# Output projection's first two tiles: the half of their products that reads the recurrence's and the delta rule's features is moved into the block before

## The chip, the cores and the metric

The kernel runs on one core of one Trainium2 chip. The metric is the device time in microseconds (us) of the whole program, median of three runs. TensorE (PE in the rows, PEld for its weight loads) multiplies; VectorE (DVE), ScalarE (ACT), GpSimd (POOL) and the DMA queue of SyncE (SP) work beside it.

## The reference, cut to what matters

Two decoder layers over 512 prompt tokens and 8 sequences of 4 sample tokens, width 1024, all in float32. Each layer computes

```python
z = x @ w_in                       # split among four mixers of 256 columns each
y_m = mLSTM, y_r = retention       # chunked mixers; each ends in a head norm and a gate
y_g = RG-LRU, y_w = RWKV-7         # linear recurrence; delta rule
mix = concat([y_m, y_r, y_g, y_w]) @ w_out
x = layer_norm(ALPHA * x + mix)    # then cross attention and a squared-ReLU MLP, alike
```

The row of `mix` of one token is a sum over 1024 features. 512 of them are the chunked mixers' (A is mLSTM, B retention), 256 the linear recurrence's (C), 256 the delta rule's (D).

## The kernel before, in words

Each layer is written as two blocks of five instruction streams, one for each engine. A block ends for all engines together: none begins the next block's stream before the last has ended the former's. Semaphores order the work inside a block.

The first block makes the features. They lie transposed, feature on the partition and the 544 tokens along the row, in eight tiles of 128 features: `Y = [z(f) for f in (6, 7, 14, 15, 18, 19, 20, 21)]`. Indices 0 and 1 are A's, 2 and 3 B's, 4 and 5 C's, 6 and 7 D's. C's and D's tiles are final when the semaphores `yC` and `yD` are up, D's during the loop over the chunks of A and B. The block's end on TensorE is the transpose of some state columns (L1143), then `head_means` and `head_variances` of A and B, each a product with a matrix of 1/64 (the helper's line is L585). Behind them ScalarE takes the eight variance halves out of PSUM with a logarithm (L1620) and makes the inverse roots (L1739), and VectorE multiplies A's and B's heads with them and with their gains and gates (L1569, L1571). Nothing else is left to do in the block then.

The second block begins with `project_tensor`. `w_out` is in the weight ring by then, as slabs 11 and 12, one for each half of 512 output columns. First it multiplies the 32 sample tokens (`part`, L1998): eight products for each half, four of which lie beside each other in groups of 32 columns of the array. Then come the four tiles of 128 prompt tokens (T0 to T3), for each half eight products of 128x128 by 128x512 that are summed in one PSUM bank (L2006). A float32 product is two records in the trace. Behind T0 the sample rows are folded (L2012); behind T1, T2 and T3 earlier tiles are transposed as soon as VectorE has normalised them (`turn_x_tensor`, L313). VectorE adds `ALPHA * x` to each half as its bank is full (`residual`, L2042), takes the moments (L287, L291) and normalises in two steps (L295, L297). It needs x back for that: SyncE's queue loads it at the start of the second block from the output tensors where the first block had parked it (L2631, L2632), then the norm's gain and bias (L323, L324), and then keys and values for the attention.

PSUM has eight banks; `bk.begin` waits until the bank's last reader has given it back. The variances of A lie in banks 0 to 3, those of B in banks 4 to 7.

Of the kernel before, what the change touches and what calls it, by code (L numbers as in the profile page):

```python
# [12 lines left out]
KC = D // P  # L13
DEPTH = 2
SEQ = 512
NB = 8
TS = 4
NS = NB * TS
NT = SEQ + NS
# [6 lines left out]
W512 = 512  # L26
# [13 lines left out]
TILES = [(0, 128), (128, 128), (256, 128), (384, 128), (SEQ, NS)]  # L40
# [179 lines left out]
def build(nc, A, O, table, where):  # L220

    with ExitStack() as ctx:
# [8 lines left out]
        tmp = sb("tmp", TMP)  # L231
# [3 lines left out]
        psum = ctx.enter_context(nc.psum_tensor("psum", [P, 8, 512], F32))  # L235

        def const(name, *shape):
            a, n = where[name]
            v = con[:, a:a + n]
            if len(shape) == 2:  # L240
                v = v.rearrange("p (a b) -> p a b", a=shape[0])
            return v

        def cols(t, at, *shape):
            n = 1
            for s in shape:
                n *= s
            v = t[:, at:at + n]
            if len(shape) == 2:
                v = v.rearrange("p (a b) -> p a b", a=shape[0])  # L250
            if len(shape) == 3:
                v = v.rearrange("p (a b c) -> p a b c", a=shape[0], b=shape[1])
            if len(shape) == 4:
                v = v.rearrange("p (a b c d) -> p a b c d", a=shape[0], b=shape[1], c=shape[2])
            return v

        def z(f, n=1):
            v = big[:, f * NT:(f + n) * NT]
            return v if n == 1 else v.rearrange("p (n t) -> p n t", n=n)
# [6 lines left out]
        wring = cols(ring, 0, 2, KC, W512)  # L266
# [39 lines left out]
        def turn_x_tensor(pe, bk, sig, ln, T, at, banks):  # L306

            t0, n = TILES[T]
            pe.wait_ge(sig["ln_done"], 5 * ln + at + 1)
            for g in range(2):  # L310
                ps = bk.begin(pe, ("xT", ln, T, g), banks[g]).rearrange("p (c t) -> p c t", c=4)
                for c in range(4):
                    ins = pe.transpose(ps[:, c, :n], xk[:n, T, (4 * g + c) * P:(4 * g + c + 1) * P], ident[:n, :n])  # L313
                bk.filled(ins, ("xT", ln, T, g))
# [34 lines left out]
        sig = Signals(nc, ctx, "")  # L349
        bk = Banks(sig, psum)  # L350
        for l in range(DEPTH):
            sig.layer()
            bk.layer()
            LN0, LN1, LN2, LN3 = range(3 * l, 3 * l + 4)
# [201 lines left out]
            def slab_wait(eng, n):  # L556

                if n < 2:
                    eng.wait_ge(sig[f"first{n}"], 16 * (l + 1))
                elif n == 17:  # L560
                    eng.wait_ge(sig["slab_up"], sig.at("slab_up", 16))
                else:
                    eng.wait_ge(sig[f"slab{n % 2}"], sig.at(f"slab{n % 2}", 16 * (n // 2 - (n > 17 and n % 2))))


            def slab_pe(pe, n):

                slab_wait(pe, n)
                return up_first if n == 17 else wring[:, n % 2, :, :]
# [144 lines left out]
                sp.dma_start(con[:, n_first:], table[:, n_first:]).then_inc(sig.dma("con"), 16)  # L714


            with nc.Block() as block:

                @block.tensor
                def _(pe):  # L720
# [9 lines left out]
                    ps = bk.begin(pe, ("prow",), 4)  # L730
                    bk.filled(pe.transpose(ps[:, :N_ROWS], prow[:N_ROWS, :], ident[:N_ROWS, :N_ROWS]), ("prow",))
                    ps = bk.begin(pe, ("prow2",), 5)
                    bk.filled(pe.transpose(ps[:, :64], prow2[:64, :], ident[:64, :64]), ("prow2",))
                    pe.wait_ge(sig["Sraw"], sig.at("Sraw", 16 * NB))
                    for pr in range(2):
                        ps = bk.begin(pe, ("SsT", pr), 6 + pr).rearrange("p (b c) -> p b c", b=4)
                        for b4 in range(4):
                            ins = pe.transpose(ps[:, b4, :], Sraw[:, b4, 2 * pr:2 * pr + 2, :].rearrange("p a b -> p (a b)"), ident)
# [3 lines left out]
                    if l == 0:  # L742
                        pe.wait_ge(sig["mem"], 16)
                        for nt in range(2):
                            for g in range(2):
                                ps = bk.begin(pe, ("memT", nt, g), 6 + g).rearrange("p (c t) -> p c t", c=4)
                                for c in range(4):
                                    k = 4 * g + c
                                    ins = pe.transpose(ps[:, c, :], mems[:, nt, k * P:(k + 1) * P], ident)
# [29 lines left out]
                    ps = bk.begin(pe, ("orow1",), 6)  # L779
# [11 lines left out]
                    for T in range(5):  # L791
                        t0, n = TILES[T]
                        pe.wait_ge(sig["dfeat"], sig.at("dfeat", 1))
                        for i, pair in enumerate(((X2, X4), (z(ZK_D, 2), z(ZV_D, 2)))):
                            ps = bk.begin(pe, ("dtok", T, i), 4 + i).rearrange("p (a c) -> p a c", a=4)
                            for j in range(2):
                                for pr in range(2):
                                    ins = pe.transpose(ps[:n, 2 * j + pr, :], pair[j][:, pr, t0:t0 + n], ident)
# [4 lines left out]
                        for i, left in enumerate((X4, z(ZK_D, 2))):  # L803
                            if i:
                                spare_products(pe, ("dsc", T), 4, (0, 1))
                            ps = bk.begin(pe, ("dsc", T, i), 6 + i).rearrange("p (q a s t) -> p q a s t", q=2, a=2, s=2)
                            for pr in range(2):
                                for c in own_chunks:
                                    tc = slice(t0 + c.start, t0 + c.stop)
                                    w = c.stop - c.start  # L810
                                    ins = pe.matmul(ps[c, pr, :, :, :w], left[:, pr, tc], dpad[:, pr, :, :, c], start=True, stop=True)
# [3 lines left out]
                        for li, m in enumerate(levels):  # L815
# [3 lines left out]
                            ps = bk.begin(pe, ("X", T, m), 2)[:, 0:256].rearrange("p (h t) -> p h t", h=H)  # L819
# [3 lines left out]
                            for h in range(H):  # L823
                                for c in own_chunks:
                                    w = c.stop - c.start
                                    ins = pe.matmul(ps[c, h, :w], om[c, h, :w], (const("ident64") if m == 1 else Dm[:, h, :])[c, :w],
                                                    start=True, stop=True)
# [5 lines left out]
                            if not last:  # L833
                                ps = bk.begin(pe, ("D", T, m), 3)[:, 0:256].rearrange("p (h t) -> p h t", h=H)
                                for h in range(H):
                                    for c in own_chunks:
                                        w = c.stop - c.start
                                        ins = pe.matmul(ps[c, h, :w], DmT[c, h, :w], Xm[c, h, :w], start=True, stop=True)
                                bk.filled(ins, ("D", T, m))
                            ps = bk.begin(pe, ("DT", T, m), 4)[:, 0:256].rearrange("p (h t) -> p h t", h=H)  # L840
                            for h in range(H):
                                for c in own_chunks:
                                    w = c.stop - c.start
                                    ins = pe.matmul(ps[c, h, :w], Xm[c, h, :w], DmT[c, h, :w], start=True, stop=True)
# [4 lines left out]
                        ps = bk.begin(pe, ("CV", T), 6)[:, 0:256].rearrange("p (h v) -> p h v", h=H)  # L849
# [7 lines left out]
                        if T < 4:  # L857
# [8 lines left out]
                            ps = bk.begin(pe, ("UV", T), 7)[:, 0:256].rearrange("p (h v) -> p h v", h=H)  # L866
# [125 lines left out]
                    def head_variances(pre, sq, bank):  # L992

                        pe.wait_ge(sig[pre + "sq"], sig.at(pre + "sq", 1))
                        for i in range(2):
                            product(pe, (pre + "var", i), bank + i, lambda k: sq[:, i, :], [const("mean64")])
# [148 lines left out]
                    head_means("B", z(ZQ_B, 2), 4)  # L1145
                    head_variances("A", X2, 0)
                    head_variances("B", X4, 4)


                @block.vector  # L1150
# [830 lines left out]
            up_first = cols(big, 16 * NT + 4096, KC, W512)  # L1981
            KEY_BANKS = (0, 1, 3)
            pvs = cols(tmp, 10260, W256)
            Y = [z(f) for f in (6, 7, 14, 15, 18, 19, 20, 21)]


            partial = cols(tmp, 10698, 2, W512)
            PROJ_ORDER = (0, 4, 1, 2, 3)


            def project_tensor(pe, pre, left, slabs, ln):

                w = [slab_pe(pe, n) for n in slabs]
                for half in range(2):
                    ps = bk.begin(pe, (pre, "part", half), half)
                    for k in range(KC):
                        g = (k % 4) * NS
                        ins = pe.matmul(ps[g:g + NS, :], left[k][:, SEQ:NT], w[half][:, k, :], start=(k < 4), stop=(k >= 4),  # L1998
                                        skip_group_check=True)
                    bk.filled(ins, (pre, "part", half))  # L2000
                for T in range(4):
                    t0, n = TILES[T]
                    for half in range(2):
                        ps = bk.begin(pe, (pre, T, half), 2 * ((T + 1) % 2) + half)
                        for k in range(KC):
                            ins = pe.matmul(ps[:n, :], left[k][:, t0:t0 + n], w[half][:, k, :], start=(k == 0), stop=(k == KC - 1))  # L2006
                        bk.filled(ins, (pre, T, half))
                    if T == 0:
                        for half in range(2):
                            bk.given(pe, (pre, "part", half))  # L2010
                            ps = bk.begin(pe, (pre, 4, half), 6 + half)
                            bk.filled(pe.matmul(ps[:NS, :], const("fold"), partial[:, half, :], start=True, stop=True), (pre, 4, half))  # L2012
                    if T == 1:
                        turn_x_tensor(pe, bk, sig, ln, 0, 0, (4, 5))
                    if T == 2:
                        turn_x_tensor(pe, bk, sig, ln, 4, 1, (4, 5))
                        turn_x_tensor(pe, bk, sig, ln, 1, 2, (4, 5))
                    if T == 3:
                        turn_x_tensor(pe, bk, sig, ln, 2, 3, (4, 5))


            def project_scalar(s, pre, ln):
# [272 lines left out]
            with nc.Block() as block:  # L2295

                @block.tensor
                def _(pe):
                    project_tensor(pe, "wout", Y, (11, 12), LN1)

                    pe.wait_ge(sig["kpt"], sig.at("kpt", 16))
                    for nt in range(2):
# [431 lines left out]
```

## Time and profile before

| what | us |
|---|---|
| median of the runs (2537.10 to 2543.14) | 2538.28 |
| the profiled execution | 2533.99 |
| its span, first to last instruction | 2532.0 |
| TensorE busy in it | 2406.4 |
| idle time of TensorE ahead of the projection, layer 0 | 9.05 |
| the same, layer 1 | 9.04 |

A time at the left of a timeline row counts from the start of the span. A row shows its start, its length, engine, line and operation, what it writes and reads, and how many records it joins; the bracket is the idle time before it and what ended it. In a row of stretches each engine has its busy time and its records in brackets; the clock beside them is 1.00 for TensorE's 2.4 GHz and 0.50 for 1.2 GHz.

### The profile page before, as it was taken

The page shows a single profiled execution, that of the slowest core. Times are in us where ns is not written, and L with a number is a line of the kernel's source. Part 1 is how long each engine was busy: PE and PEld are TensorE (multiplying, and loading weights), DVE is VectorE, ACT ScalarE, POOL GpSimd, SP SyncE. Part 2 cuts the span into 40 slices and gives each one's busy share as a digit, 9 for nine tenths or more (in the row PEclk, how much of TensorE's full clock was granted, in tenths as well). Part 3 has the DMA queues.
Part 4 walks back from the last instruction along what each step waited for, and adds up shares of the span by engine and source line. Part 5 has one row for each costly group of instructions (what it writes and reads, how often), then busy time and mean ns, then how long its engine had stood idle before and what let it go on. Part 6 is the DMA issues. An engine that isn't in the chain of part 4 may idle for free. (4 is left out here: it accounts for less than half of the span.)

```text
span 2532.0 us, 31605 instructions
## 1 busy us (share of the span) xinstructions
PE 2406.4 (95%) x13470; PEld 1761.3 (70%) x13470; DVE 811.9 (32%) x1617; ACT 465.6 (18%) x983; POOL 110.9 (4%) x208
## 2 busy tenths in 40 slices
PE   7989998979999999999989899989899999999997
PEld 6867674545874888888877666655458658888886
DVE  4242233544033644000132422436321345430012
ACT  2331122011121222000023321220112212220000
POOL 0011100100000000000001011000000000000000
PEclk9999998979999999999999999989799999999999
DMA  7111003253233112222231111023433331212220
GB/s 268 64 37 36 6 30 88 72 175 117 106 140 135 65 67 100 67 67 67 68 117 67 34 36 35 23 86 100 139 133 112 139 133 40 94 67 90 77 67 36
DMA packets 137674, 215.05 MB, mean 85 GB/s; under 512 B 35528, under 2 KB 69632, under 8 KB 137408
## 3 DMA queue, kind: packets, MB, share of 16 engines
q1 hardware_dynamic: 135232, 208.84, 24.4%
q10 hardware_dynamic: 2304, 4.20, 0.4%
q8 instruction: 108, 1.77, 0.3%
q14 instruction: 30, 0.25, 0.0%
HBM read 198.43 MB, written 14.58 MB: 84 GB/s over the span
## 5 line engine op out<-in xcount | busy, mean ns | idle before, releaser
L2137 PE MATMUL psum<-big,ring 128*128 128x288 f32 (+1 forms) x2048 | 471.2, 393 | 0.0
L2137 PEld LDWEIGHTS psum<-big,ring 128*128 128x128 f32 x2048 | 388.5, 190 | 79.9 <-DMA ring<-in_w_down 0.4
L585 PE MATMUL psum<-xT,ring 128*128 128x256 f32 (+1 forms) x1536 | 357.8, 394 | 8.4 <-DMA ring<-in_w_in 6.0
L585 PEld LDWEIGHTS psum<-xT,ring 128*128 128x128 f32 x1536 | 291.9, 191 | 69.8 <-DMA ring<-in_w_in 6.2
L632 PE MATMUL psum<-xT,ring 128*128 128x256 f32 (+1 forms) x768 | 223.5, 418 | 0.1
L2080 PE MATMUL psum<-tmp 128*128 128x272 f32 x768 | 181.4, 393 | 0.0
L2080 PEld LDWEIGHTS psum<-tmp 128*128 128x128 f32 x768 | 145.8, 190 | 30.8 <-issue 0.8
L632 PEld LDWEIGHTS psum<-xT,ring 128*128 128x128 f32 x768 | 134.3, 192 | 41.4 <-issue 15.2
L331 DVE SCALAR_TENSOR_TENSOR xtok<-xtok,psum 128x256 f32<-128x256 f32 (+1 forms) x40 | 16.3, 407 | 442.4 <-PE psum L2071 421.3
L629 PE MATMUL psum<-ring,ext 128*128 128x512 f32 x256 | 120.0, 610 | 4.5 <-ACT ext L1600 4.5
L2412 PE MATMUL psum<-ring,big 128*128 128x512 f32 x256 | 113.1, 595 | 0.0
L2006 PE MATMUL psum<-ring,big 128*128 128x512 f32 x256 | 111.6, 594 | 0.0
L2080 PE MATMUL psum<-xT,ring 128*128 128x272 f32 x448 | 107.2, 392 | 0.0
L1593 ACT ACTIVATE big<-psum 128x256 f32<-128x256 f32 (+1 forms) x112 | 44.4, 396 | 320.5 <-PE psum L585 197.2
L2080 PEld LDWEIGHTS psum<-xT,ring 128*128 128x128 f32 x448 | 85.0, 190 | 17.4
L2265 ACT ACTIVATE tmp<-psum 128x256 f32<-128x256 f32 (+1 forms) x32 | 12.7, 398 | 450.5 <-PE psum L2137 450.5
L2006 PEld LDWEIGHTS psum<-ring,big 128*128 128x128 f32 x256 | 48.0, 190 | 60.8 <-issue 60.8
L629 PEld LDWEIGHTS psum<-ring,ext 128*128 128x128 f32 x256 | 47.5, 194 | 58.6 <-issue 54.7
L2412 PEld LDWEIGHTS psum<-ring,big 128*128 128x128 f32 x256 | 47.4, 190 | 56.9 <-issue 56.9
L2042 DVE SCALAR_TENSOR_TENSOR xtok<-xtok,psum 128x512 f32<-128x512 f32 (+1 forms) x40 | 27.3, 682 | 140.4 <-PE psum L2006 86.5
L2080 PE MATMUL psum<-xT,tmp 128*128 128x272 f32 x256 | 63.9, 392 | 0.0
L2242 ACT ACTIVATE big<-psum 128x272 f32<-128x272 f32 x32 | 12.7, 398 | 267.8 <-PE psum L2080 267.8
(449 smaller groups left out, 2693.8 us busy)
## 6 DMA issues: line engine op xcount, KB each, us to landing
ring<-in_w_down SPq DMA_DIRECT2D x16, 2048.0 KB, 8.2
ring<-in_w_in SPq DMA_DIRECT2D x14, 2048.0 KB, 8.5
ring<-in_w_up SPq DMA_DIRECT2D x14, 2048.0 KB, 7.9
big<-in_cache_mem_k SPq DMA_DIRECT2D x16, 1024.0 KB, 5.4
ring<-in_xa_wk SPq DMA_DIRECT2D x4, 2048.0 KB, 8.1
ring<-in_xa_wv SPq DMA_DIRECT2D x4, 2048.0 KB, 10.1
ring<-in_w_out SPq DMA_DIRECT2D x4, 2048.0 KB, 8.9
tmp<-in_cache_mem_v SPq DMA_DIRECT2D x8, 1024.0 KB, 10.0
```

The lines of the kernel that those rows point to most:

```text
L331: ins = v.scalar_tensor_tensor(x, x, ALPHA, ps[:n, (T % 2) * W256:(T % 2) * W256 + W256], ALU.mult, ALU.add)
L585: ins = pe.matmul(ps[:m, :w], lhsT_list[k], rhs(k)[:, c], start=(k == 0), stop=(k == n - 1))
L629: ins = pe.matmul(bank, memT[:, k, half * P:(half + 1) * P], wring[:, n % 2, k, :], start=(k == 0), stop=(k == KC - 1))
L632: ins = pe.matmul(bank[:, :c.stop - c.start], wring[:, n % 2, k, i * P:(i + 1) * P], xTv[:, k, c], start=(k == 0), stop=(k == KC - 1))
L1593: bk.give(act(z(f)[:, c], ps[:, 0:c.stop - c.start], fn, scale=scale), ("z", f, half))
L2006: ins = pe.matmul(ps[:n, :], left[k][:, t0:t0 + n], w[half][:, k, :], start=(k == 0), stop=(k == KC - 1))
L2042: bk.give(v.scalar_tensor_tensor(x, x, ALPHA, ps[:n, :], ALU.mult, ALU.add), key)
L2080: ins = pe.matmul(ps[:, :HT], left[:, k, :], right[:, k, :], start=(k == 0), stop=(k == KH - 1))
L2137: ins = pe.matmul(ps, w[r][:, k, i * P:(i + 1) * P], hT[:, 2 * KC * r + k, c], start=(r == 0 and k == 0), stop=(r == 1 and k == 2 * KC - 1))
L2242: bk.give(s.activation(hT[:, 2 * u + 1, T_HALVES[0]], ps[:, :HT], ACT.Copy), ("up", u, 0))
L2265: bk.give(s.activation(yT[q % 2][:, i, c], ps[:, :c.stop - c.start], ACT.Copy), ("down", q, i, half))
L2412: ins = pe.matmul(ps, aT[:, k, t0:t0 + n], w[:, k, :], start=(k == 0), stop=(k == KC - 1))
```

## The change

The order of the work on TensorE changes, and the banks. `wout_ahead` is called at the end of the first block, behind `head_variances`: for T0 and T1, both halves, it multiplies the features 4 to 7 (C and D) and leaves the sums open in their banks. In the second block `wout_tensor` takes the place of `project_tensor`: `part` first, then for T0 and T1 the features 0 to 3 that are still missing, and T2 and T3 with all eight, 4 to 7 first. The folds and transposes keep their places between the tiles. T0 and T2 use banks 2 and 3, T1 and T3 banks 0 and 1, `part` banks 4 and 5 (before: 0 and 1). No product is added or left out, and the streams of the other engines are as they were.

```diff
+            WOUT_BANKS = ((2, 3), (0, 1), (2, 3), (0, 1))
+            def wout_tile(pe, T, ks):
+                t0, n = TILES[T]
+                for half in range(2):
+                    w = wring[:, (11 + half) % 2]
+                    key = ("wout", T, half)
+                    if key not in bk.turn:
+                        bk.begin(pe, key, WOUT_BANKS[T][half])
+                    ps = psum[:, bk.turn[key][0], :]
+                    for k in ks:
+                        ins = pe.matmul(ps[:n, :], Y[k][:, t0:t0 + n], w[:, k, :], start=(k == 4), stop=(k == 3))
+                    if ks[-1] == 3:
+                        bk.filled(ins, key)
+
+            def wout_ahead(pe):
+                for half in range(2):
+                    slab_wait(pe, 11 + half)
+                pe.wait_ge(sig["yC"], sig.at("yC", 1))
+                pe.wait_ge(sig["yD"], sig.at("yD", 1))
+                for T in range(2):
+                    wout_tile(pe, T, range(4, KC))
+
+            def wout_tensor(pe):
+                for half in range(2):
+                    ps = bk.begin(pe, ("wout", "part", half), 4 + half)
...
+                for T in range(4):
+                    wout_tile(pe, T, range(4) if T < 2 else (4, 5, 6, 7, 0, 1, 2, 3))
...
                     head_variances("A", X2, 0)
                     head_variances("B", X4, 4)
+                    wout_ahead(pe)
...
-                    project_tensor(pe, "wout", Y, (11, 12), LN1)
+                    wout_tensor(pe)
```

## Rows read from the trace of the kernel before

**Rows 1.** The page's first part: busy time, share of the span, instructions.

```profile
PE 2406.4 (95%) x13470; PEld 1761.3 (70%) x13470; DVE 811.9 (32%) x1617; ACT 465.6 (18%) x983; POOL 110.9 (4%) x208
```

**Rows 2.** Timeline of TensorE's products in layer 0.

```profile
540.97 3.99 PE L585 MATMUL psum<-tmp,con 128*128 128x256 f32 x16
554.01 6.09 PE L1998 MATMUL psum<-ring,big 128*32 128x512 f32 x32 [9.05 <-PEq L717]
560.03 14.00 PE L2006 MATMUL psum<-ring,big 128*128 128x512 f32 x32
573.96 1.91 PE L2012 MATMUL psum<-tmp,con 128*32 128x512 f32 x4
575.79 14.00 PE L2006 MATMUL psum<-ring,big 128*128 128x512 f32 x32
```

**Rows 3.** Timeline of all engines in layer 0's idle time.

```profile
542.71 4.12 ACT L1620 ACTIVATE tmp<-psum,con 128x256 f32<-128x256 f32 x8
...
552.05 1.48 DVE L1571 SCALAR_TENSOR_TENSOR big<-big,tmp 128x544 f32<-128x544 f32 x2
553.82 0.40 SPq L2631 DMA_DIRECT2D xtok<-out_y_prompt  x1
```

**Rows 4.** Timeline of TensorE's products in layer 1.

```profile
1798.78 1.08 PE L585 MATMUL psum<-tmp,con 128*128 128x256 f32 x4
1808.89 5.00 PE L1998 MATMUL psum<-ring,big 128*32 128x512 f32 x32 [9.04 <-PEq L717]
1813.82 14.00 PE L2006 MATMUL psum<-ring,big 128*128 128x512 f32 x32
```

**Rows 5.** Stretches of 1 us: PE, PEld, DVE, ACT, POOL, clock, DMA share, GB/s.

```profile
549.00:550.00 1.00, 0.00 (x0) 0.00 (x0) 0.96 (x2) 0.00 (x0) 0.00 (x0) 0.50 0.00 0
...
559.00:560.00 1.00, 1.00 (x12) 0.13 (x4) 0.00 (x0) 0.00 (x0) 0.00 (x0) 1.00 1.05 430
...
1804.00:1805.00 1.00, 0.00 (x0) 0.00 (x0) 0.96 (x3) 0.00 (x0) 0.00 (x0) 0.93 0.00 0
...
1811.00:1812.00 1.00, 1.00 (x9) 0.24 (x5) 0.00 (x0) 0.00 (x0) 0.00 (x0) 0.66 0.91 348
```

**Rows 6.** DMA packets between 545 and 554 us.

```profile
DMA packets 0, 0.00 MB, mean 0 GB/s; under 512 B 0, under 2 KB 0, under 8 KB 0
```

**Rows 7.** TensorE around the border between the layers.

```profile
1266.14 0.82 PE L2071 MATMUL psum<-con,tmp 128*128 128x128 f32 x6
1272.92 8.57 PE L585 MATMUL psum<-xT,ring 128*128 128x256 f32 x32 [5.96 <-DMA ring<-in_w_in]
```

**Rows 8.** SyncE's queue in layer 0, ahead of the idle time.

```profile
502.64 10.07 SPq L404 DMA_DIRECT2D ring<-in_w_out  x2
```

**Rows 9.** SyncE's queue in layer 1, the second block's start.

```profile
1809.14 0.50 SPq L2632 DMA_DIRECT2D xtok<-out_y_sample  x1
...
1810.15 1.23 SPq L324 DMA_DIRECT2D tmp<-in_ln_b  x1
```

**Rows 10.** DMA issues in the same stretch: count, size, us to landing.

```profile
tmp<-in_ln_b SPq DMA_DIRECT2D x1, 512.0 KB, 10.8
xtok<-out_y_sample SPq DMA_DIRECT2D x1, 128.0 KB, 9.4
```

**Rows 11.** Timeline of VectorE at T0's second half, layer 0.

```profile
574.14 0.69 DVE L2042 SCALAR_TENSOR_TENSOR xtok<-xtok,psum 128x512 f32<-128x512 f32 x1 [6.18 <-PE psum L2006]
574.86 1.29 DVE L287 BATCH_NORM_STATS2 sm<-xtok 128x6 f32<-128x512 f32 x2
576.18 0.21 DVE L291 BATCH_NORM_AGGREGATE sm<-sm 128x2 f32<-128x12 f32 x1
576.43 1.28 DVE L295 SCALAR_TENSOR_TENSOR xtok<-xtok,sm,tmp 128x1024 f32<-128x1024 f32 x1
577.75 1.28 DVE L297 SCALAR_TENSOR_TENSOR xtok<-xtok,sm,tmp 128x1024 f32<-128x1024 f32 x1
```

**Rows 12.** Behind the projection: the second pair of key transposes, layers 0 and 1.

```profile
624.47 1.97 PE L2307 MATMUL psum<-con,tmp 128*128 128x128 f32 x8 [2.70 <-ACT big L2553]
...
1878.26 1.15 PE L2307 MATMUL psum<-con,tmp 128*128 128x128 f32 x8 [2.69 <-ACT big L2553]
```

**Rows 13.** Stretches of 2 us in layer 0, columns as in rows 5.

```profile
518.00:520.00 2.00, 2.00 (x4) 0.37 (x3) 1.03 (x2) 0.00 (x0) 0.00 (x0) 0.50 1.05 410
...
624.00:626.00 2.00, 1.53 (x7) 1.54 (x8) 1.03 (x1) 1.28 (x3) 0.00 (x0) 0.50 1.05 401
```

More of the change, by code:

```diff
@@ L714, in first_loads @@
                 sp.dma_start(con[:, n_first:], table[:, n_first:]).then_inc(sig.dma("con"), 16)
+            Y = [z(f) for f in (6, 7, 14, 15, 18, 19, 20, 21)]
+            partial = cols(tmp, 10698, 2, W512)
+            WOUT_BANKS = ((2, 3), (0, 1), (2, 3), (0, 1))
[11 more added lines that the diff above has]
+                        bk.filled(ins, key)
@@ new lines, in wout_ahead @@
+            def wout_ahead(pe):
[8 more added lines that the diff above has]
+                    ps = bk.begin(pe, ("wout", "part", half), 4 + half)
+                    for k in range(KC):
+                        g = (k % 4) * NS
+                        ins = pe.matmul(ps[g:g + NS, :], Y[k][:, SEQ:NT], wring[:, (11 + half) % 2, k, :], start=(k < 4), stop=(k >= 4),
+                                        skip_group_check=True)
+                    bk.filled(ins, ("wout", "part", half))
+                for T in range(4):
+                    wout_tile(pe, T, range(4) if T < 2 else (4, 5, 6, 7, 0, 1, 2, 3))
+                    if T == 0:
+                        for half in range(2):
+                            bk.given(pe, ("wout", "part", half))
+                            ps = bk.begin(pe, ("wout", 4, half), 6 + half)
+                            bk.filled(pe.matmul(ps[:NS, :], const("fold"), partial[:, half, :], start=True, stop=True), ("wout", 4, half))
+                    if T == 1:
+                        turn_x_tensor(pe, bk, sig, LN1, 0, 0, (4, 5))
+                    if T == 2:
+                        turn_x_tensor(pe, bk, sig, LN1, 4, 1, (4, 5))
+                        turn_x_tensor(pe, bk, sig, LN1, 1, 2, (4, 5))
+                    if T == 3:
+                        turn_x_tensor(pe, bk, sig, LN1, 2, 3, (4, 5))
@@ L1983, in build @@
             pvs = cols(tmp, 10260, W256)
-            Y = [z(f) for f in (6, 7, 14, 15, 18, 19, 20, 21)]
-            partial = cols(tmp, 10698, 2, W512)
             PROJ_ORDER = (0, 4, 1, 2, 3)
[L1991 to L2019, printed above, removed]
             def project_scalar(s, pre, ln):
```

## The prediction

> **What bounds the kernel.** I read the busy shares first: TensorE works 95% of the span, no other engine over 32% [rows 1]. So time is TensorE's products plus the places where it stands, and a reordering pays only where it fills such a place. Next the timeline of TensorE around the edited code. In layer 0 the variances end at 540.97 + 3.99 = 544.96, and the projection's first product starts at 554.01, after 9.05 us idle, released by the end of the block and not by data [rows 2]. Layer 1 repeats it with 9.04 us [rows 4]. Then the other engines in that gap: ScalarE takes the eight variance halves until 546.83, and VectorE's last gate product ends at 552.05 + 1.48 = 553.53; the first instruction of the next block, a load, follows at 553.82 [rows 3]. The chain of head norms therefore sets the gap, and TensorE has no part in it after 544.96.
>
> Last the stretches of 1 us, for the clock. It stands at 0.50 (1.2 GHz) from 549.00 and is back at 1.00 (2.4 GHz) from 559.00; in layer 1 it falls near 1804.9 and is back near 1811.7 (the 0.66 of that stretch is 0.68 us low and 0.32 us full) [rows 5]. So the first products after the gap run at half speed: the gap costs more than its length.
>
> **What is removed, moved and added.** Moved are 2 tiles x 2 halves x 4 features = 16 products, 32 records. T0's 32 records before start at 560.03 and what follows them starts at 573.96: 13.93 us [rows 2]. The same number of records now stands at the end of the first block, in each layer.
>
> *Do they start at once?* They need three things. The weights: both `w_out` slabs were issued between 502.64 and 512.7, over 30 us ahead [rows 8]. The features C and D: D's last write lies in the chunk loop, before the means. And free banks: T0 takes 2 and 3, which ScalarE drains as second and fourth of its eight reads, 4.12 / 8 = 0.515 us each, so at 542.71 + 1.03 = 543.74 and 544.77; the product that wants bank 2 comes at 544.96, the one for bank 3 half a tile (3.5 us) later [rows 2, 3]. I cost the start at nothing.
>
> *The end of the block.* TensorE now ends last, at 544.96 + 13.93 = 558.9, where VectorE still ends at 553.53: its chain hangs on the variances, which are issued before the moved products. The 9.05 us disappear, and the overhang of 4.9 us is work that has left the second block, so it costs nothing. What stays is the border itself. Its price with TensorE as the last engine is in no row. Below: 0.29 us, from VectorE's end to the next load [rows 3]. Above: TensorE's own end at 1266.14 + 0.82 = 1266.96 to its next product at 1272.92, 5.96 us, put down to a weight load [rows 7]. VectorE's end to TensorE's start was 0.48 us; the case is nearest to that one, and I take 0.6.
>
> A rule speaks for the upper end. The Trainium skill, "Runtime: NRT & Kernel Launch", section on instruction fetch mechanics, says that a taken branch to a page that isn't loaded stalls the engine until a DMA has brought it. In the old order such a fetch could have hidden in the 9 us. The trace speaks against it: between 545 and 554 not one DMA packet moves, instruction queues included [rows 6]. The page gives no time for such a stall, so by it the sum would only be worse by an unstated amount, between my two bounds.
>
> *The clock.* `part` took 560.03 - 554.01 = 6.02 us in layer 0, of which 5.0 low: at full clock 2.5 + 1.0 = 3.5. In layer 1 it took 4.93 us, of which 2.8 low: 1.4 + 2.1 = 3.5 too [rows 2, 4, 5]. With TensorE standing for 0.6 us in place of 9, behind 13.9 us of wide products, I expect the clock to stay at 2.4 GHz. Gain 2.5 us and 1.4 us; bound on the other side nothing.
>
> *The reload, which is now late.* All loads of the second block start behind the border, some 5.4 us later than before, while `part` and T0 are shorter by 2.5 + 7 us. Take S as the block's first product. T0's first half is full at S + 3.5 + 3.5 = S + 7. The sample rows of x are issued 0.25 us after S and land 9.4 us later, S + 9.65; the norm's bias 1.26 us after S and 10.8 us later, S + 12.1 (layer 1, the later one) [rows 4, 9, 10]. VectorE so waits some 3 us for x, which it didn't before. The second half is full at S + 10.5, and from its residual add to the end of the norm it is 577.75 + 1.28 - 574.14 = 4.9 us [rows 11]: S + 15.5. TensorE asks for T0's transposes after `part` 3.5, T0 7.0, fold 1.8 (573.96 to 575.79) and T1 7.0, at S + 19.3. So 3.8 us are left and I cost the reload at nothing. If the loads were later than that, each us would be a us, at this transpose. T4 and T1 come up behind T2's 14 us, T2 behind T3's 14: as before. The attention's weights are released by T3, its first keys are wanted 60 us in; they move with TensorE.
>
> *Banks in the second block.* `part` takes 4 and 5, free since 546.9; T2 takes T0's, read by VectorE at S + 11.3, long before. Nothing.
>
> **Sum.** Layer 0: 9.05 + 2.5 - 0.6 = 10.95. Layer 1: 9.04 + 1.4 - 0.6 = 9.85. Together 20.8 us. The profiled execution took 2533.99 us (2532.0 of span and 2.0 around it), so 2513.2. The median of the runs shown stands 4.3 us above that execution; the same offset gives 2517.5.
>
> **Rivals.**
> - *The border costs more when TensorE ends last* (code fetched, drain). For: no row shows it, and the rule above. Against: the empty DMA stretch. At its bound, 5.96 in place of 0.6 twice, 10.7 us are lost: 2528. From 3 us each on it is 2522. Chance 0.08.
> - *The clock gives nothing back*, since it falls anyway around the border. For: in layer 0 a wait of 2.70 us was enough for 0.50 at 624 to 626, and the transposes there took 1.97 us, which in layer 1 took 1.15 [rows 12, 13]. Against: the pause is now 0.6. Then 3.9 us are missing: 2521.5. Chance 0.07.
> - *The gap reappears at T0's transpose*, because x comes late. It begins when the norm is over 3.8 us later than worked out; at some 14 us later in each layer the gain is gone and the time is the old one, beyond it slower. For: the loads are the only thing that starts later. Against: landings of 9.4 and 10.8 us are measured ones under the same load. Partial stall 0.03, no change 0.02.
> - *The other side: the clock is low under the moved products.* A busy TensorE doesn't suffice: at 518 to 520 it was busy throughout, with narrow products, at 0.50 [rows 13]. At 1.2 GHz the moved records would take 27.9 us and `part` 7.0. Per layer the piece from the variances to T0's old length is then 27.9 + 0.6 + 7.0 = 35.5 against 9.05 + 6.02 + 13.93 = 29.0, or 28.0 in layer 1: 14 us slower in all, 2552. It decides from about 21 us of low clock in a layer. Against: these products are 128x512 over the full array, and the 64 records of T0 and T1 took 14.00 us each, at full clock. Chance 0.02.
>
> The forecast itself has 0.78. Within it: the border from 0.29 to 2 us, and the clock's falls elsewhere (a shift of all that follows can add or take one, some 1 us each), with the spread of the median (2537.1 to 2543.1): 2512 to 2522. To hold 8 in 10 with the bounds I give 2511 to 2526, which takes in the clock rival and most of the border's. Less than 0.3% (7.6 us), about what a measurement of this kernel can tell from no change, needs a loss of 13 us out of 20.8: same 0.03, slower 0.02, faster 0.95.
>
> **What would show it.** In the profile after: products of the projection directly behind the variances, 13.9 us, without a wait; an idle time of about 0.6 us at the block's end; clock 1.00 through `part`, which takes 3.5 us; VectorE's first residual add waiting for the load; T0's transposes without idle time before them; all later groups as before. It is wrong if the border takes over 2 us, if a stretch at 0.50 lies in `part` or in the moved products, or if a wait stands before T0's transposes.

## The result and the profile after

| | median us | runs | ratio to before, 95% interval |
|---|---|---|---|
| before | 2539.20 | 6 | |
| changed | 2519.79 | 6 | 0.9921 [0.9905, 0.9936] |
| changed, second set | 2522.88 | 5 | 0.9933 [0.9920, 0.9947] |
| changed, third set | 2522.56 | 5 | 0.9924 [0.9909, 0.9938] |

The change is 17 to 20 us faster, clear of noise in all three sets. The forecast was 2517.5 us in a range of 2511 to 2526, and a sum of 20.8 us, a ratio of 0.9918.

The timeline of TensorE's products in layer 0 after the change answers to [rows 2]. The moved and the remaining products of the prompt tiles are L732 now, the sample rows L753, the fold L762, and the border of the blocks L772.

```profile
546.95 4.00 PE L585 MATMUL psum<-tmp,con 128*128 128x256 f32 x16
550.78 13.89 PE L732 MATMUL psum<-ring,big 128*128 128x512 f32 x32
564.98 3.64 PE L753 MATMUL psum<-ring,big 128*32 128x512 f32 x32 [0.30 <-PEq L772]
568.55 7.13 PE L732 MATMUL psum<-ring,big 128*128 128x512 f32 x16
575.61 1.91 PE L762 MATMUL psum<-tmp,con 128*32 128x512 f32 x4
577.45 7.13 PE L732 MATMUL psum<-ring,big 128*128 128x512 f32 x16
584.42 1.04 PE L313 MATMUL psum<-con,xtok 128*128 128x128 f32 x8
```

The 32 moved records follow the variances without a wait. At the border TensorE stands 0.30 us in place of 9.05, and the sample rows take 3.64 us in place of 6.09. Below, the piece of a layer is the stretch from the variances' first record to tile 0's transposes. In layer 0 it was 589.63 - 540.97 = 48.66 us and is 584.42 - 546.95 = 37.47; in layer 1 it was 47.75 and is 37.46. The ends of the pieces of before that [rows 2, 4] don't hold are these, layer 0 first:

```profile
589.63 1.04 PE L313 MATMUL psum<-con,xtok 128*128 128x128 f32 x8
...
1795.67 4.18 PE L585 MATMUL psum<-tmp,con 128*128 128x256 f32 x16
...
1843.42 1.04 PE L313 MATMUL psum<-con,xtok 128*128 128x128 f32 x8
```

Layer 1 of the changed kernel has the same picture as its layer 0:

```profile
1792.85 3.99 PE L585 MATMUL psum<-tmp,con 128*128 128x256 f32 x16
1796.68 13.89 PE L732 MATMUL psum<-ring,big 128*128 128x512 f32 x32
1810.87 3.64 PE L753 MATMUL psum<-ring,big 128*32 128x512 f32 x32 [0.30 <-PEq L772]
...
1830.31 1.04 PE L313 MATMUL psum<-con,xtok 128*128 128x128 f32 x8
```

The stretches of 1 us around the border, which answer to [rows 5]: the clock stays at 1.00 throughout.

```profile
564.00:565.00 1.00, 0.70 (x6) 0.05 (x5) 0.00 (x0) 0.06 (x1) 0.00 (x0) 1.00 0.00 0
565.00:566.00 1.00, 1.00 (x12) 0.45 (x16) 0.00 (x0) 1.00 (x1) 0.00 (x0) 1.00 0.00 0
...
568.00:569.00 1.00, 1.00 (x9) 0.30 (x2) 0.00 (x0) 0.32 (x1) 0.00 (x0) 1.00 1.03 418
```

VectorE in the same layer, against [rows 3, 11]. Its last gate product still ends ahead of the border, now by 5 us; its first residual add waits for the load of x and no longer for the product.

```profile
558.02 1.48 DVE L1627 SCALAR_TENSOR_TENSOR big<-big,tmp 128x544 f32<-128x544 f32 x2
574.08 0.69 DVE L2065 SCALAR_TENSOR_TENSOR xtok<-xtok,psum 128x512 f32<-128x512 f32 x1 [14.57 <-DMA xtok<-out_y_sample]
575.80 0.69 DVE L2065 SCALAR_TENSOR_TENSOR xtok<-xtok,psum 128x512 f32<-128x512 f32 x1 [1.04 <-PE psum L732]
...
579.41 1.28 DVE L297 SCALAR_TENSOR_TENSOR xtok<-xtok,sm,tmp 128x1024 f32<-128x1024 f32 x1
```

Tile 0 is normalised at 580.69, 3.7 us before its transposes are asked for at 584.42.

One thing doesn't fit at first sight: the two pieces gained 11.2 and 10.3 us, and yet this profile's span is 2520.7 us against 2532.0, only 11.3 less. The rest lies where the code was not changed. The first profile of before came to layer 0's variances at 540.97, this one at 546.95, and the stretches of the chunk loop show why. The rows are TensorE's busy time, records and so on, with the clock third from the end; the first fence is of the kernel before, the second of the changed one.

```profile
227.00:231.00 4.00, 4.00 (x26) 2.96 (x25) 0.69 (x1) 1.09 (x2) 0.39 (x1) 1.00 0.00 0
199.00:365.00 166.00, 159.86 (x1881) 115.74 (x1880) 38.20 (x99) 34.91 (x88) 21.08 (x38) 1.00 0.08 27
```

```profile
227.00:231.00 4.00, 4.00 (x19) 2.42 (x17) 0.00 (x0) 1.17 (x2) 0.00 (x0) 0.57 0.00 0
199.00:365.00 166.00, 159.86 (x1742) 114.19 (x1741) 36.22 (x94) 32.51 (x84) 21.05 (x38) 0.96 0.08 27
```

TensorE is busy alike, but at 0.96 of the clock it gets through fewer records in 166 us. That stretch ends 186 us ahead of the first moved product (550.78), so the product itself can't have caused it; whether it belongs to the changed kernel or to the execution is for the further profiles below to say.

### The profile page after: what moved, and what is told of

The parts are those of the page before. It is cut to its first block and busy times, and to the rows that moved or that the text cites. A ratio compares the mean times of both kernels' runs of the same rounds, so it can differ in the third digit from the quotient of the medians.

```text
span 2520.7 us, 31607 instructions
## 1 busy us (share of the span) xinstructions
PE 2412.5 (96%) x13470; PEld 1765.9 (70%) x13470; DVE 812.1 (32%) x1617; ACT 466.0 (18%) x983; POOL 110.7 (4%) x208
## 5 line engine op out<-in xcount | busy, mean ns | idle before, releaser
L585 PE MATMUL psum<-xT,ring 128*128 128x256 f32 (+1 forms) x1536 | 360.5, 396 | 8.4 <-DMA ring<-in_w_in 5.9
L585 PEld LDWEIGHTS psum<-xT,ring 128*128 128x128 f32 x1536 | 293.9, 192 | 70.6 <-DMA ring<-in_w_in 6.2
L632 PE MATMUL psum<-xT,ring 128*128 128x256 f32 (+1 forms) x768 | 228.2, 425 | 0.1
L632 PEld LDWEIGHTS psum<-xT,ring 128*128 128x128 f32 x768 | 137.6, 196 | 43.2 <-issue 16.1
L629 PE MATMUL psum<-ring,ext 128*128 128x512 f32 x256 | 119.3, 607 | 4.5 <-ACT ext L1656 4.5
L732 PE MATMUL psum<-ring,big 128*128 128x512 f32 x256 | 111.9, 594 | 0.0
L2103 PEld LDWEIGHTS psum<-xT,ring 128*128 128x128 f32 x448 | 85.0, 190 | 17.4
L732 PEld LDWEIGHTS psum<-ring,big 128*128 128x128 f32 x256 | 48.0, 190 | 60.0 <-issue 59.8
L629 PEld LDWEIGHTS psum<-ring,ext 128*128 128x128 f32 x256 | 47.5, 194 | 58.5 <-issue 54.7
```

Source lines behind the costliest of these rows:

```text
L585: ins = pe.matmul(ps[:m, :w], lhsT_list[k], rhs(k)[:, c], start=(k == 0), stop=(k == n - 1))
L629: ins = pe.matmul(bank, memT[:, k, half * P:(half + 1) * P], wring[:, n % 2, k, :], start=(k == 0), stop=(k == KC - 1))
L632: ins = pe.matmul(bank[:, :c.stop - c.start], wring[:, n % 2, k, i * P:(i + 1) * P], xTv[:, k, c], start=(k == 0), stop=(k == KC - 1))
L732: ins = pe.matmul(ps[:n, :], Y[k][:, t0:t0 + n], w[:, k, :], start=(k == 4), stop=(k == 3))
L2103: ins = pe.matmul(ps[:, :HT], left[:, k, :], right[:, k, :], start=(k == 0), stop=(k == KH - 1))
```

## The experiments

All ratios are against the kernel before, run on the same chip in the same rounds.

**The changed kernel again**, as a yardstick.

> The changed kernel once more, as the yardstick of this set. By the measured pieces of its first profile (11.2 us gained in layer 0 and 10.3 us in layer 1 between the variances and the transposes of tile 0) it is 20 to 21.5 us faster than the kernel before, ratio 0.9915 to 0.9925. If the four extra low-clock stretches in each layer's chunk loop of that profile belonged to the change and not to chance, they show again and the gain is nearer 11 us, 0.9957.

Measured 2522.88 us, 0.9933 [0.9920, 0.9947]. The pieces are 37.66 us in both layers. The chunk loop from 199 to 365 us ran at 1.00 this time:

```profile
199.00:365.00 166.00, 159.86 (x1858) 115.15 (x1856) 38.96 (x100) 32.59 (x85) 21.78 (x39) 1.00 0.08 27
```

So the extra low stretches of the first profile don't belong to the change. A kernel that moves nothing has them as well: the one with products for nothing (below) had 0.96 there.

**The same order behind the border.** The call is taken out of the first block and put at the start of the second.

```diff
                     head_variances("B", X4, 4)
-                    wout_ahead(pe)
...
             def wout_tensor(pe):
+                wout_ahead(pe)
```

> The same order and the same banks, but the 16 products stand behind the border of the blocks, as the first thing of the second block. The theory (the gain is the idle time ahead of the border): TensorE stands 9.05 us again and starts at 1.2 GHz, the time is that of the kernel before, ratio 0.998 to 1.002. The rival (the gain comes from the new order or the banks in the second block): 20 us faster here too, 0.992.

Measured 2544.70 us, 1.0022 [1.0012, 1.0032]. The gain is gone, so it comes from the place and neither from the order of the features nor from the banks. It is even 5.6 us slower than before (3.0 to 8.1 by the interval), just outside the expected 0.998 to 1.002. The timeline shows why:

```profile
559.25 17.01 PE L732 MATMUL psum<-ring,big 128*128 128x512 f32 x32 [9.30 <-PEq L773]
576.18 3.64 PE L754 MATMUL psum<-ring,big 128*32 128x512 f32 x32
```

The restart at 1.2 GHz now falls on the wide products, 17.01 us in place of 13.9, while the sample rows behind them take 3.64 us in place of 6.09 and 5.00. The pieces are 49.86 and 49.72 us, 1.2 and 2.0 more than in the first profile of before, and 2.0 and 1.9 more than in its second one. Together that is 3.2 or 3.9 us, which lies within the interval of the time.

**One layer only.** In layer 0 the call stands ahead of the border, in layer 1 behind it.

```diff
                     head_variances("B", X4, 4)
-                    wout_ahead(pe)
+                    if l == 0:
+                        wout_ahead(pe)
...
             def wout_tensor(pe):
+                if l:
+                    wout_ahead(pe)
```

> The products are ahead of the border in layer 0 alone, in layer 1 behind it. The theory: the layers add up, 11.2 us of gain, ratio 0.9955. The rival (the shift of everything behind layer 0 gives or takes as much as the place): anything from 0.992 to 0.999.

Measured 2533.73 us, 0.9968 [0.9956, 0.9980], 8.1 us (5.1 to 11.2). The pieces are 37.65 us in layer 0, as with the change, and 48.78 in layer 1: 11.0 gained and 1.0 lost against the first profile of before, 10.0 together. The expected 11.2 us had left out the loss in the layer in which the products stand behind the border. In the pieces the layers add up; the time alone allows that and the rival too, whose range (0.992 to 0.999) it lies in.

**One tile only.** Tile 0's products are ahead, tile 1 is computed whole in the second block.

```diff
-                for T in range(2):
+                for T in range(1):
                     wout_tile(pe, T, range(4, KC))
...
-                    wout_tile(pe, T, range(4) if T < 2 else (4, 5, 6, 7, 0, 1, 2, 3))
+                    wout_tile(pe, T, range(4) if T < 1 else (4, 5, 6, 7, 0, 1, 2, 3))
```

> Only tile 0's eight products, 6.95 us, are ahead. They fit in the 9.05 us, so VectorE ends the block again, at its old time. The theory: 6.95 us less behind the border in each layer, and the pause of some 2.6 us leaves the clock at 2.4 GHz, which gives the 2.5 and 1.4 us of the sample rows: 13.9 + 3.9 = 17.8 us faster, ratio 0.9930. If the clock falls in a pause of 2.6 us as well: 13.9 us, 0.9945. The rival (more moved is more gained in proportion): half of the change's gain, 10 us, 0.996.

Measured 2524.88 us, 0.9943 [0.9931, 0.9956], 14.5 us.

```profile
551.13 7.03 PE L732 MATMUL psum<-ring,big 128*128 128x512 f32 x16
560.17 3.64 PE L753 MATMUL psum<-ring,big 128*32 128x512 f32 x32 [2.02 <-PEq L772]
```

Half the products leave 2.02 us of idle time and the clock is kept all the same. The pieces are 39.38 and 39.37 us, 9.3 and 8.4 gained: 17.7, as the theory has it. Proportional gain (10 us) is out. The time of the whole program (interval 11 to 17.5 us) agrees with them only at its edge, and its ratio is nearer to the 0.9945 expected for a clock that falls. So it does not decide by itself whether the clock paid; the profile does, with 3.64 us for the sample rows in both layers.

**Products for nothing.** The kernel before, with eight wide products whose sum nobody reads, behind the variances.

```diff
                     head_variances("B", X4, 4)
+                    slab_wait(pe, 12)
+                    bk.given(pe, ("Avar", 0, 1))
+                    for k in range(KC):
+                        pe.matmul(psum[:, 2, :], z(18 + k % 4)[:, 0:P], wring[:, 0, k, :], start=True, stop=True)
```

> The kernel before, with eight 128x128 by 128x512 products (7 us) added at the end of the first block; nobody reads their result, and no work is moved. It measures the clock's part by itself. If the clock is a gain of its own, the sample rows take 3.6 us in place of 6.0 and 4.9: 3.8 us faster, ratio 0.9985. If only the idle time counts, or the clock falls anyway at the border: 1.0000.

Measured 2538.99 us, 0.9994 [0.9984, 1.0004].

```profile
554.06 7.03 PE L1151 MATMUL psum<-ring,big 128*128 128x512 f32 x16
563.25 3.64 PE L2002 MATMUL psum<-ring,big 128*32 128x512 f32 x32 [2.17 <-PEq L717]
```

In the profile the clock's part is there by itself: the sample rows take 3.64 us with no work removed, and the pieces are 46.20 and 46.39 us, 2.5 and 1.4 less than in the first profile of before. In the time of the whole program 3.8 us can't be told from nothing here: the interval reaches from 4.1 us faster to 1.0 slower.

**Three tiles.** Tile 2's second half of features goes ahead as well; its sums take banks 4 and 5, and `part` and the transposes behind T1 and T2 move to 6 and 7.

```diff
-            WOUT_BANKS = ((2, 3), (0, 1), (2, 3), (0, 1))
+            WOUT_BANKS = ((2, 3), (0, 1), (4, 5), (0, 1))
...
-                for T in range(2):
+                for T in range(3):
                     wout_tile(pe, T, range(4, KC))
```

> Tile 2's eight products are ahead as well, 7 us more in the first block in each layer. The theory: the gap is already full with two tiles, so nothing more is gained and the larger overhang costs nothing; tile 1's transposes are asked for 28.4 us into the second block and its norm is done at 26.7, so no new wait. As fast as the change, 20 to 21 us faster than before, 0.992. The rival (what is moved is gained): 34 us, 0.9865. The other rival (the overhang delays the loads and VectorE's later tiles): slower than the change by the wait, some us in each layer.

Measured 2520.65 us, 0.9914 [0.9901, 0.9928], within two of the three intervals of the change and overlapping the third. From the variances to tile 1's transposes it is 53.06 us in both layers, to 0.01 us what the first profile of the change has. With the gap full, 7 us more ahead of the border bring nothing and cost nothing:

```profile
551.42 20.76 PE L732 MATMUL psum<-ring,big 128*128 128x512 f32 x48
572.48 3.64 PE L753 MATMUL psum<-ring,big 128*32 128x512 f32 x32 [0.30 <-PEq L772]
```

**The reload late.** In SyncE's queue the keys and the first two value loads go ahead of x and of the norm's parameters.

```diff
-                    sp.dma_start(xk[:, 0:4, :], yp).then_inc(sig.dma("xres"), 16)
-                    sp.dma_start(xk[:NS, 4, :], ys).then_inc(sig.dma("xres"), 16)
...
                     v_load(0)
                     v_load(1)
+                    sp.dma_start(xk[:, 0:4, :], yp).then_inc(sig.dma("xres"), 16)
+                    sp.dma_start(xk[:NS, 4, :], ys).then_inc(sig.dma("xres"), 16)
```

The two loads of `ln_params` move with them.

> The changed kernel, with 3 MB of keys and values issued ahead of the reload of x and of the norm's parameters in SyncE's queue. At the 410 GB/s of the profile x lands 7.7 us later. In the profile of the change the norm of tile 0 is done 3.7 us before its transposes are asked for. The theory (slack of 3.7 us, then each us is a us): 4.0 us of wait in each layer, 8 us slower than the change, 12 us faster than before, 0.9953. The rival (the reload is hidden anyway): as the change, 0.992.

Measured 2528.92 us, 0.9949 [0.9937, 0.9962], 13 us faster than before and so 4 to 7 slower than the change. VectorE's first residual add starts at 581.17 in place of 574.08, 7.1 us later into the block, and 7.6 us later in layer 1. Now tile 0's transposes wait:

```profile
587.61 1.97 PE L313 MATMUL psum<-con,xtok 128*128 128x128 f32 x8 [3.03 <-DVE xtok L297]
589.37 15.94 PE L732 MATMUL psum<-ring,big 128*128 128x512 f32 x32
...
1834.40 1.09 PE L313 MATMUL psum<-con,xtok 128*128 128x128 f32 x8 [2.43 <-DVE xtok L297]
1835.33 13.90 PE L732 MATMUL psum<-ring,big 128*128 128x512 f32 x32
```

The waits are 3.03 and 2.43 us, less than the 4.0 expected. With the change the second half's add still stood 1.04 us (layer 0) and 1.36 us (layer 1) for its product after x had come; here it doesn't, so a late x can use that time besides the 3.7 us. That makes 4.8 and 5.1 us of slack; in layer 0 the norm then lost 0.81 us to its bias, which had been moved back with x. In layer 0 the clock fell behind the wait as well, and tile 2 took 15.94 us in place of 13.90. So the slack is real: beyond it a late reload is waited for, and may take the clock with it.

**One half earlier.** Four of the moved products, tile 0's first half, are issued while TensorE waits for VectorE in A's decode states; they take bank 7, and B's means and variances alternate in two banks to leave it free.

```diff
                         elif T == 4:
+                            if pre == "A":
+                                wout_early(pe)
...
-                        product(pe, (pre + "mu", i), bank + i, lambda k: ht[:, i, :], [const("mean64")])
+                        product(pe, (pre + "mu", i), bank + (i if pre != "B" else 0), lambda k: ht[:, i, :], [const("mean64")])
```

> The changed kernel, with four of the moved products (tile 0, first half) issued earlier still, where TensorE waits 2.10 us for VectorE's masked values of A's decode states; B's means and variances use two banks in turn in place of four. The theory: another 2.1 us of idle time is filled in each layer, and the norm chain, which ends 5 us before TensorE at the border, can take the delay: 4 us faster than the change, more if the wide products lift the clock there (0.50 for 24 us): 0.990 to 0.988. The rival: the norm chain becomes the later one again and gives it back, 0.992.

Measured 2519.06 us, 0.9911 [0.9897, 0.9924]: by the time alone not to be told from the change, nor from the 0.990 expected. The profile speaks against a gain.

```profile
515.02 2.82 PE L629 MATMUL psum<-ring,ext 128*128 128x512 f32 x6
...
531.76 6.60 PE L732 MATMUL psum<-ring,big 128*128 128x512 f32 x8
538.29 1.07 PE L1171 MATMUL psum<-big,tmp 32*64 32x512 f32 x4
540.23 2.21 PE L1171 MATMUL psum<-big,tmp 32*64 32x512 f32 x4 [0.86 <-DVE big L1570]
...
554.57 1.29 PE L585 MATMUL psum<-tmp,con 128*128 128x256 f32 x4 [1.26 <-ACT tmp L1683]
```

The 2.10 us wait is filled, but the eight records run almost wholly at 1.2 GHz there, 6.60 us in place of 3.5, and two new waits of 0.86 and 1.26 us come behind them. From the last value products (L629) to tile 0's transposes (585.90) layer 0 takes 70.88 us; with the change it is 515.45 to 584.42, 68.97. Layer 1 loses 1.9 us too (70.86 for 68.96). The norm chain does not end last either (the border's wait is still 0.30), so the rival's reason fails as well. Whether the theory of a gain fails stays open: the profiled execution is the slowest of the five (2522.82 us) and has the lowest granted clock (0.973), while the other four took 2515.88 to 2520.89 us at 0.976 to 0.977, more than any of the 16 executions of the changed kernel had (0.970 to 0.975). No profile shows where the clock was higher in them.

**Both kernels beside each other once more.**

> The kernel before under another name: a second profile of it, and what two equal kernels differ by in this measurement. Ratio 1.000, within 0.0015. Its piece from B's and A's variances to the transposes of tile 0 is 48.7 and 47.7 us again, give or take 1 us for the clock of the sample rows. If the first profile's 541 us up to there were luck, this one is nearer the 545 to 550 us of the other profiles.

Measured 2539.14 us, 0.9999 [0.9990, 1.0008]. Its pieces are 47.85 and 47.86 us. Here the clock was low for less of layer 0's sample rows than in [rows 2]:

```profile
558.37 5.09 PE L1998 MATMUL psum<-ring,big 128*32 128x512 f32 x32 [9.04 <-PEq L717]
```

And it came to layer 0's variances at 545.15, not at 540.97; from 199 to 365 us the clock was 0.98. So the same kernel differs by 4 us there from one execution to the next.

> The changed kernel beside the copy of the kernel before. By the pieces it is 21.5 us faster, 0.9915; by the two measurements so far 17 to 19.5 us, 0.9927. Its piece from the variances to the transposes of tile 0 is 37.5 us in both layers. What is missing between the two is in the chunk loops, where the clock falls now in one place and now in another, and not in the projection.

Measured 2522.56 us, 0.9924 [0.9909, 0.9938], with 37.66 us in both layers and the variances at 545.81. Against the copy of before the pieces gain 10.19 and 10.20 us, 20.4 together; against the first profile it was 21.5. The measurements say 17 to 20 us. Part of what is missing can be placed: from tile 0's transposes in layer 0 to the variances of layer 1 the two profiles of before take 1206.0 and 1205.0 us, the three of the changed kernel 1208.4, 1208.2 and 1208.4. The stretch is long, and the code in it is the same. With three tiles ahead it has no such loss: from tile 1's transposes to layer 1's variances that kernel takes 1190.1 us, the kernel before 1190.5 and 1189.4, the changed kernel 1192.6 to 1192.8. So having products ahead does not bring the loss by itself; its cause stays open.

**The next gap.** Behind the projection stands the same kind of idle time: TensorE waits 2.7 us for a bank of the key transposes [rows 12], since ScalarE, in its order, waits for tile 3's moments first. ScalarE's norm step is put between the two pairs of key transposes.

```diff
                 turn_x_scalar(s, bk, sig, ln, 1)
-                ln_scalar(s, sig, ln, 3, 4)
                 turn_x_scalar(s, bk, sig, ln, 2)
...
                     for nt in range(2):
+                        if nt:
+                            ln_scalar(s, sig, LN1, 3, 4)
                         for g in range(2):
```

> The changed kernel with ScalarE's order changed behind the projection: it drains tile 2's transposes and the first pair of the key transposes before it waits for tile 3's moments, where it now waits with both behind it and TensorE stands 2.69 us for a bank. The theory (the same kind of gap, idle time that one engine's order makes for another): the wait falls to about 0.8 us in each layer, 3.8 us faster than the change, and some us more where the clock no longer falls behind it. The rival: tile 3's norm comes later and is waited for at its own transposes, no gain.

Measured 2513.08 us, 0.9891 [0.9876, 0.9905], the fastest of the study, 9.5 us below the changed kernel of the same set.

```profile
615.07 1.04 PE L2329 MATMUL psum<-con,tmp 128*128 128x128 f32 x8
616.46 1.15 PE L2329 MATMUL psum<-con,tmp 128*128 128x128 f32 x8 [0.35 <-ACT big L2577]
617.44 7.07 PE L585 MATMUL psum<-xT,ring 128*128 128x256 f32 x32
```

The wait fell from 2.70 to 0.35 us in both layers, 4.7 us, and the clock did not fall behind it; tile 3's transposes came without a wait too, so the rival fails. The queries' first products take 7.07 us, against 8.52, 7.07 and 7.07 in layer 0 and 8.49, 7.07 and 8.76 in layer 1 of the three profiles of the change, on average 0.8 us more in a layer. That explains some 6 us of the 9.5. The rest lies within the two intervals.

## Why the prediction held

*The gap and its filling.* Right. The start cost nothing: no wait for banks, weights or features stands before the moved records, which took 13.89 us for 13.93. Behind the border the same products bring nothing (1.0022), ahead of it in one layer about half (0.9968), and beyond the gap's length nothing more (0.9914 with three tiles). The gain is idle time filled, and its limit is the gap.

*The border.* Taken at 0.6 us, between 0.29 and 5.96; it is 0.30 in every profile in which TensorE ends last. This term was off by 0.3 us in each layer. The rule of the Trainium skill ("Runtime: NRT & Kernel Launch", instruction fetch mechanics), by which a branch to a page that isn't loaded stalls the engine, doesn't show here: with no gap to hide in, TensorE stood 0.30 us, and from 563 to 566 us of the profile after not one DMA packet moved.

*The clock.* Right in the profiles: 3.64 us for 3.5 forecast, at 1.00 throughout. The kernel with products for nothing shows the term alone, 2.5 and 1.4 us against the first profile of before. Against the copy of before the sample rows gain 1.5 and 1.3 us, so the term depends on the execution: 3.8 us in one profile of before and 2.8 in the other, for 3.9 forecast. It is the term that was sized from too few rows: one profile of before, in which the clock was low for longer in layer 0. No time of a whole program shows it apart from noise.

*The reload.* Right: the first add at 9.1 us into the block (forecast 9.65), norm done at 15.7 (15.5), transposes asked for at 19.4 (19.3), slack 3.7 us (3.8). Delayed by 7.1 and 7.6 us it costs waits of 3.03 and 2.43 us. It is the resource that the change spent: before, the norm was done at 579.03 [rows 11], 10.6 us ahead of the transposes at 589.63.

*The rivals.* A dear border, a clock that falls anyway, a gap that reappears at tile 0's transposes, low clock under the moved products: none occurred in any of the three profiles of the changed kernel.

*The sum.* 20.8 us forecast; the pieces measure 20.4 to 21.5, the whole program 17 to 20 in three sets, each with an interval that reaches 20 us or more. The profiles of the changed kernel lose 2.2 to 3.4 us between the two pieces, in unchanged code; the forecast has no term for that, and its cause stays open. The forecast median, 2517.5 us, adds the offset of one execution of before (4.3 us) to the sum. That this comes within 2.3 us of the measured 2519.79 is in part luck, since the part of the program ahead of layer 0's variances alone differs by 4 us between two executions of before.

## What to carry to other kernels

At a border where all engines meet, look which engine's chain ends last and for how long the bound engine stands; products whose inputs are ready can be taken ahead if their sums may stay open in banks that the waiting chain has given back. The gain is the gap, not what is moved, and here half the work already kept the clock at 1.00 (sample rows in 3.64 us). Look then at what the border releases (here the reload of x): it starts later while its reader comes sooner, and the slack between them is the price of the next step.

## What the runs showed that was not expected

The same instructions in the same order get a different clock from execution to execution: from 199 to 365 us, in the chunk loop, the mean was 1.00, 0.98, 0.96, 1.00 and 1.00 in five profiles of the two kernels, and layer 0's variances began at 541.0 to 547.1 us. A single profiled span is therefore no measure of a gain of 20 us: 11.3 us between the first two profiles, against 20.4 to 21.5 in the pieces that the change touches. Behind a wait of 2.7 us the clock was low in some executions and not in others (1.15 to 1.97 us for the same transposes); behind pauses of 2.0 to 2.2 us between dense products it was not, in the four cases seen.

Wide products did not lift the clock at once: issued at 531.76 us with the early half, they ran their first 5.9 us at 0.50. It then stood at 1.00 for 3.4 us, and from 541.1 to 547.9 at 0.50 again. In every other profile it stands at 0.50 in this part without a break, for 24 us in each layer, though TensorE is far from idle there: in the first profile of the changed kernel it is busy for 20.66 us from 521 to 545.
